# A two-layer streaming encoder trunk on one core: when the last output tiles, the late modulation sums and the layer norm's mean work are handed between the engines

## The reference, cut to what matters

```python
for layer in range(2):
    mod = silu(c) @ ada_w[layer] + ada_b[layer]
    sh1, sc1, g1, sh2, sc2, g2 = split(mod, 6)
    h = rmsnorm(x, norm_g[layer, 0]) * (1 + sc1) + sh1
    y = diff_attention(h) if layer == 0 else conformer_conv(h)
    x = x + g1 * y
    h = rmsnorm(x, norm_g[layer, 1]) * (1 + sc2) + sh2
    x = x + g2 * conv_ffn(h)
return rmsnorm(x, final_g)

def conformer_conv(h):
    a = h @ w_pw1 + b_pw1
    a = a[..., :1024] * sigmoid(a[..., 1024:])
    a = causal_dwconv(a, w_dw) + b_dw          # 31 taps for each channel
    a = silu(layernorm(a, ln_g, ln_b))
    return a @ w_pw2 + b_pw2
```

## Time and profile before

| what | us |
|---|---|
| median of 3 runs | 1253.19 |
| lowest and highest run | 1252.7, 1255.36 |
| the profiled execution | 1246.89 |
| its span | 1245.1 |
| TensorE busy in it | 1211.5 (97%) |
| VectorE, ScalarE, POOL busy | 708.4, 543.3, 541.5 |
| mean granted clock of TensorE | 0.982 of full speed |

### The profile page before, as it was taken

The page is one execution under the profiler, slowest core; times in us unless marked ns, Lnnn a source line. Parts: engine busy times, 40 slices in busy tenths (PEclk is TensorE's granted clock), DMA queues, the critical chain, the costliest instruction groups (busy, mean ns, idle before and its releaser), DMA issues.

```text
span 1245.1 us, 16710 instructions
## 1 busy us (share of the span) xinstructions
PE 1211.5 (97%) x5454; PEld 968.8 (78%) x5454; DVE 708.4 (57%) x1166; ACT 543.3 (44%) x872; POOL 541.5 (43%) x273
## 2 busy tenths in 40 slices
PE   7999999989999999999999999999999999999996
PEld 6877777767888888888888776577888888888885
DVE  5677767864767633347887899962533333340002
ACT  4356555544434434342224666753544444442221
POOL 2433323124344434454443799743444444454440
PEclk6899999899999999999999999999999999999998
DMA  9844443222655433336673212012223332222321
GB/s 358 245 143 143 152 168 118 102 102 68 203 184 171 150 102 101 101 112 228 241 241 107 85 68 68 34 39 97 83 86 101 101 101 101 91 104 93 103 83 68
DMA packets 45639, 157.04 MB, mean 126 GB/s; under 512 B 5536, under 2 KB 5792, under 8 KB 45600
## 3 DMA queue, kind: packets, MB, share of 16 engines
q1 hardware_dynamic: 44928, 156.21, 37.1%
q10 hardware_dynamic: 672, 0.34, 0.1%
HBM read 154.10 MB, written 2.42 MB: 126 GB/s over the span
## 4 chain that ended last, share of the span: by engine, by line
PE 79%; DVE 13%; issue 3%; ACT 2%; DMA 1%; POOL 1%; SPq 0%; DVEq 0%; POOLq 0%; ACTq 0%
PE psum L937 24%; PE psum L938 24%; PE psum L939 24%; DVE psum L1786 6%; PE psum L948 1%; DVE pt_lo L1516 1%; DVE psum L1507 1%; PE psum L971 1%; PE psum L1096 1%; DMA ada_first<-ada_w 1%; DVE acc L1358 1%; POOL acc_p L522 1%; PE psum L960 0%; PE psum L1123 0%; DMA w_raw<-w_tiles 0%
## 5 line engine op out<-in xcount | busy, mean ns | idle before, releaser
L509 POOL TENSOR_TENSOR w_lo<-w_raw,w_hi 128x1024 fp32r<-128x1024 f32 (+1 forms) x192 | 455.9, 2391 | 653.6 <-ACT w_hi L596 653.6
L937 PE MATMUL psum<-h_hi,w_hi 128*128 128x512 f32 x1152 | 462.1, 401 | 7.0 <-DVE x L1615 2.2
L938 PE MATMUL psum<-h_lo,w_hi 128*128 128x512 f32 x1152 | 451.4, 392 | 0.0
L939 PE MATMUL psum<-h_hi,w_lo 128*128 128x512 f32 x1152 | 451.3, 392 | 0.0
L937 PEld LDWEIGHTS psum<-h_hi,w_hi 128*128 128x128 f32 x1152 | 218.4, 190 | 56.7 <-issue 9.6
L939 PEld LDWEIGHTS psum<-h_hi,w_lo 128*128 128x128 f32 x1152 | 217.8, 189 | 46.5
L938 PEld LDWEIGHTS psum<-h_lo,w_hi 128*128 128x128 f32 x1152 | 218.1, 189 | 44.1 <-issue 1.7
L596 ACT ACTIVATE w_hi<-w_raw 128x1024 fp32r<-128x1024 f32 (+1 forms) x192 | 195.8, 1033 | 87.1 <-DMA w_raw<-w_tiles 87.0
L937 PE MATMUL psum<-a_hi,w_hi 128*128 128x512 f32 x352 | 137.1, 389 | 0.8 <-issue 0.8
L939 PE MATMUL psum<-a_hi,w_lo 128*128 128x512 f32 x352 | 136.9, 389 | 0.0
L938 PE MATMUL psum<-a_lo,w_hi 128*128 128x512 f32 x352 | 136.9, 389 | 0.0
(11 more groups left out here) (191 smaller groups left out, 1302.1 us busy)
## 6 DMA issues: line engine op xcount, KB each, us to landing
w_raw<-w_tiles SPq DMA_DIRECT2D x160, 512.0 KB, 3.3
ada_buf<-ada_w SPq DMA_DIRECT2D x32, 512.0 KB, 3.3
w_raw<-w_tiles SPq DMA_DIRECT2D x32, 448.0 KB, 3.1
ada_late<-ada_w SPq DMA_DIRECT2D x28, 512.0 KB, 5.3
ada_mid<-ada_w SPq DMA_DIRECT2D x20, 512.0 KB, 4.5
ada_first<-ada_w SPq DMA_DIRECT2D x16, 512.0 KB, 10.2
x<-x_in SPq DMA_DIRECT2D x4, 512.0 KB, 7.1
bias<-rel_scratch SPq DMA_DIRECT2D x8, 256.0 KB, 6.4
```

The costliest lines, as they stand in the source:

```text
L509: nc.gpsimd.tensor_tensor(w_lo[:, slot, 0:k], w_raw[:, (ph.tile + l) % 2, 0:k], f(w_hi[:, slot, 0:k]), ALU.subtract).then_inc(lo_done, 1)
L937: nc.tensor.matmul(dst, w_hi[:, slot, k], rhs_hi, start=first, stop=False)
L938: nc.tensor.matmul(dst, w_hi[:, slot, k], rhs_lo, start=False, stop=False)
L939: return nc.tensor.matmul(dst, w_lo[:, slot, k], rhs_hi, start=False, stop=last)
```

## The change

The constants give OUT, PW2 and the end new orders:

```diff
+LATE_ORDER, LATE_FREE = (2, 4, 1, 3), (1, 2, 3, 4, 4, 4, 5, 5)
+POOL_FINAL, FINAL_ORDER = 2, (2, 3, 0, 4, 5, 6, 1, 7)
-MORE_PE_TAPS = {4: 1, 5: 1, 6: 3, 7: 5}
+MORE_PE_TAPS = {4: 1, 5: 1, 6: 3, 7: 6}
+def pool_taps_of(t):
+    return POOL_TAPS - 1 if t == DK - 1 else POOL_TAPS
-        acc_late = at("acc_late", [P, LATE - 1, S], F32, h_base + 4 * 2 * S * 4)
+        acc_even = at("acc_even", [P, 3, S], F32, offset_of["h_lo"])
+        acc_odd = at("acc_odd", [P, 3, 3 * S], F32, offset_of["pad_v"] - 2 * 4 * 3 * S)
```

```diff
+            def last_pair(ph):
+                weights_ready(ph, 1, 1, 2)
+                for j in range(2):
+                    for k in range(DK):
+                        last = mm3(psum[:, 2 + j], slot_of(ph, 1, 2 + j), k, h_hi[:, k], h_lo[:, k], k == 0, k == DK - 1)
+                    last.then_inc(used if j else tile_used, 1)
...
-                dve.wait_ge(used, lin(i, ph.group + c + 1, 2))
+                by_tile = last and per_group == 2
+                if not by_tile:
+                    dve.wait_ge(used, lin(i, ph.group + c + 1, 2))
                 for j in range(per_group):
+                    if by_tile and j == 0:
+                        dve.wait_ge(tile_used, 1 if ph is OUT else 2)
+                    elif by_tile:
+                        dve.wait_ge(used, ph.group + 4)
```

```diff
-            attention_steps(3, 1)[14][0]()
...
             square_sum(1, 2)
-            keep_warm(12)
+            pe.wait_ge(ada_used, 8 * (CH0 + HEADS))
+            ada_product(HEAD_OUT, acc[:])
+            keep_warm(9)
```

```diff
-            for q in range(1, LATE - 1):
+            for q in LATE_ORDER:
                 last_ada(q)
...
-            last_ada(LATE - 1)
-            keep_warm(16)
+            for q in (5, 6):
+                last_ada(q)
+            keep_warm(11)
...
-                        if n == 2 and m < LATE:
-                            dve.wait_ge(ada_mm, LATE_CH + m)
+                        if n == 2:
+                            dve.wait_ge(ada_mm, LATE_CH + LATE_FREE[m - 1])
```

```diff
             act.wait_ge(delta_ready, 1)
+            nc.scalar.activation(rstd[:], delta[:], ACT.Square).then_inc(delta_squared, 1)
...
-            dve.wait_ge(delta_ready, 1)
-            V.tensor_tensor(rstd[:], delta[:], delta[:], ALU.mult).then_inc(dve_step, own.tick())
             dve.wait_ge(dsq_mm, DK)
-            dve.wait_ge(dve_step, own.now())
+            dve.wait_ge(delta_squared, 1)
...
-            late_out(LATE - 1, LATE, psum[:, LAST_OUT, 0:4])
+            late_out(5, LATE, psum[:, LAST_OUT, 0:8])
             dve.wait_ge(delta_copied, 1)
-            for m in range(DK // 2):
+            for m in range(2):
```

```diff
+            pool.wait_ge(final_gained, POOL_FINAL)
+            pool.wait_ge(rms_ready, 6)
+            for m in range(POOL_FINAL):
+                nc.gpsimd.tensor_tensor(x[:, m], x[:, m], rms[:], ALU.mult).then_inc(final_done, 1)
...
+                if n == 4:
+                    act.wait_ge(rms_ready, 5)
+                    nc.scalar.activation(rms[:], rms[:], ACT.Exp, scale=-0.5).then_inc(rms_ready, 1)
...
-                for m in range(DK):
+                for m in range(POOL_FINAL, DK):
                     V.scalar_tensor_tensor(out=x[:, m], in0=x[:, m], scalar=col("final_g", m),
```

More of the change, by code:

```diff
@@ L572, in _ @@
             pool.wait_ge(dsq_mm, DK)
-            for m in range(DK // 2, DK):
+            for m in range(2, DK):
                 nc.gpsimd.tensor_tensor(y[:, m], y[:, m], delta[:], ALU.subtract).then_inc(pool_mean, 1)
@@ L809, in residual_phase @@
                     squares(ph.bodies - 1, c, base, per_group)
+                    if ph is DOWN1 and c == 0:
+                        for m in range(POOL_FINAL):
+                            act.wait_ge(sq_ready, 4 * DK + m + 1)
+                            nc.scalar.activation(x[:, m], x[:, m], ACT.Copy, scale=col("final_g", m)).then_inc(final_gained, 1)
                     if then and c == 0:
@@ L871, in conv_group @@
                                          scale=col("w_dw", TAPS * t + tap)).then_inc(acc_started, 1)
-                for n in range(POOL_TAPS):
+                for n in range(pool_taps_of(t)):
                     b = POOL_TAPS * c + n
@@ L1645, in late_out, with head_out @@
                 dve.wait_ge(sc_read, LATE0 + MID + (1 if hi < LATE else 2))
+            def head_out():
+                dve.wait_ge(ada_mm, CH0 + HEADS)
+                at_, b = 4 * (CH0 + HEADS - 1), PARAMS["ada_b"] + 4 * (CH0 + HEADS - 1)
+                V.tensor_tensor(mod[:, at_:at_ + 4], psum[:, HEAD_OUT, 0:4], prm[:, b:b + 4], ALU.add)\
+                 .then_inc(dve_step, own.tick())
             def up(layer):
@@ L1700, in _ @@
                     residual(i, c, OUT, 0, 2, GATE[0], last=2 * i + c == 3)
+            head_out()
             norm(1)
```

45 lines of the change are left out of this document (26 added, 19 removed).

## The result

| us | before | changed |
|---|---|---|
| median of the runs | 1253.19 (1251.01 to 1257.56, 5 runs) | 1245.59 (1243.59 to 1247.62, 5 runs) |
| ratio to before, 95% interval | | 0.9934 (0.9915 to 0.9953) |
| profiled execution: time, span, mean clock | 1246.89, 1245.1, 0.982 | 1245.94, 1244.2, 0.979 |

The change makes the kernel 0.66% faster, by 7.6 us. The two profiled executions differ by only 0.95, and the first thing to explain is why: the last head's mean square, up to which nothing is changed but a few addresses, came at 264.42 before and 268.11 in the changed kernel. From there on the changed kernel took 4.6 us less. So each stretch is compared by itself, and never against the start of the span.

The account below looks back on a forecast made before the run. TensorE, busy 97% of the span, was taken as the bound, with gains only at six waits: 2.9 + 0.85 + 0.35 + 1.3 + 0.85 + 1.3 = 7.55 us, so 1253.19 - 7.55 = 1245.6 us; range 1242.0 to 1249.5.

Parts of the forecast that it names:

- A: Behind the attention: last modulation product moved behind OUT, so TensorE waits less for VectorE's first residual; 2.9 us, bounds 2.2 to 3.2.
- B: Behind OUT: last pair done tile by tile, leaving one tile's channel sum behind the last residual; 0.85 us, bounds 0.6 to 1.0.
- C: Ahead of PW1: four late products instead of five, TensorE then waits for the first `h_lo`; 0.35 us.
- D: Layer norm ahead of PW2: shorter POOL sum, square on ScalarE, fewer VectorE subtractions, Silu earlier; 1.3 us, bounds 0.3 to 1.5.
- E: Behind PW2: last pair done tile by tile as behind OUT, without the moved product; 0.85 us.
- F: Last norm and stores: VectorE does six tiles, POOL two, so the last store is issued earlier; 1.3 us, bounds 0.5 to 1.3.
- C's clock term: At PW1's start: clock falls again as before, 3.4 us at half speed losing 1.7 in both kernels; otherwise at most 1.6 gained.
- the clock gives more: Rival, 0.22: no fall at PW1, or A's gap had cost timed runs a slow stretch; gain 8.8 to 10.4, about 1243.5.
- The handovers stay: Rival, 0.20: D held by late products or a clock fall before PW2, or F's stores wait for POOL; gain 4 to 6.
- Not as it says: Rival, 0.06: earlier starts wait for loads or the convolution; only F and some of A left; gain up to 2.5.
- Slower: Rival, 0.02: clock stays at 1.2 GHz behind a new or moved wait, 20 us more at the low level; 1256.

Follow-up runs that it names:

- the second series: The changed kernel run once more without an edit, beside the kernel before: 1247.26 us (8 runs) for 1253.27, ratio 0.9955.

## Why the prediction was right, and where not

The time, 1245.6 forecast, came out at 1245.59 and, when the same kernel was run again, at 1247.26. The agreement to 0.01 is luck, as the parts show. Those behind it, from the pair of profiles:

| part | forecast | measured | |
|---|---|---|---|
| A | 2.9 | 2.83 | as worked out |
| B | 0.85 | 0.85 | as worked out |
| C | 0.35, clock as before | first product 0.29 earlier, first `u_pad` 0.93 later by a longer fall | the size of the clock's share was off |
| D | 1.3 | 1.32 | as worked out |
| E | 0.85 | 0.80 | as worked out |
| F | 1.3 | 0.0 | failed |
| sum | 7.55 | 6.1 without the clock | |

**A, B, E** went by the steps named: the product off VectorE's path, one tile's sum behind the last residual, `head_out` and its product in the shadow of the factor (the 0 that was taken for it, against up to 0.3).

**D** held link by link: last sum 0.19 earlier where 0.1 was reckoned, variance 0.64 for 0.75, Silu 1.30 for 1.35. The reading that TensorE's ninth tap leaves little of POOL's shorter sum was right, and is priced by the kernel without it: 0.32. The row was right to be set against the rule on table loads: with VectorE out of the way, Silu starts 1.41 behind the start of the load (818.00, 819.41), not 2.66. The Trainium skill, ScalarE: Activation LUTs, What ACT_TABLE_LOAD costs, has 2.66 with the drain; by it D would have given nothing, and the trace disagrees.

**F is the step that failed.** It was: "the last store is issued with the last of them, and the span ends 2.65 later. Six end 1.3 earlier, at 1241.15." The 2.65 was taken for a fixed delay behind the last issue. It is a queue: the transfer engines are full from the first store on, and the last store waits in them. From VectorE's last tile to the end it was 4.0. The last store was issued 0.76 earlier behind the first factor and landed at the same 7.62; the median landing took 2.6 us for 2.2. Nor could it be issued 1.3 earlier: by the prediction's own 0.62 from one issue to the next, eight issues that begin 0.77 behind the factor put the last at 5.1, for 5.38 before (here it came at 4.62). The rows for it were there to be asked for: the share and GB/s of the transfer engines by stretches of half a microsecond. And both bounds, 0.5 and 1.3, lay above nothing though no row excluded nothing.

**C's clock term** was of the right kind and mis-sized. Of "the clock falls again, as before: 3.4 us at half speed lose 1.7" the length held in three of the five profiles that have C's order and one-column products (19.15 to 19.39); in the other two it was 6.8 us (20.56 and 20.65). A fall of 3.4 us there cost 1.0 to 1.5 against the kernels without a fall, not 1.7, and the next 3.4 another 1.2 to 1.5. That no more than 1.6 can be had by a clock that stays up came out: 1.48 and 1.55 less than before (18.15 and 18.08).

**Why the sum still came out.** 6.1 us of parts against 7.6 between the first medians, 6.0 in the second series and 7.0 over all runs. The rival "the clock gives more" named a source for the excess: the falls behind A's gap. They exist, 1.5 to 1.6 us in four of six profiles with the empty gap and in none of the seven with part A, about 1.0 us on the mean. That would be enough for the 0.9 between 6.1 and 7.0. But the runs speak against the clock as the whole answer: the mean clock of the 13 runs of the changed kernel is 0.9788, and so is that of the 95 of before. What the falls behind A's gap gave back may have been lost elsewhere, as in C's longer fall, and then they explain no excess. Where the 0.9 comes from stays open. At PW2's start the clock fell in six of the eight profiles that don't have C and D both, and in two of the six that do, 1.5 us mostly; so few can't settle whether the change helps there. So the number was right by two errors that offset one another: 1.3 of F that is missing, and an excess over the parts that it didn't hold (1.5 in the first series, 0.9 over all runs, none in the second). Five parts of six hold, C's without its clock.

**The other rivals.** "The handovers stay", with a gain of 4 to 6, is touched by the second series' 6.0, but its mechanism fell with D's and B's rows; its one true piece was F, for another reason (transfers, not POOL: POOL was done at 1239.4). "Not as it says" has nothing for it. "Slower" has only C's longer fall for it, which cost 1.2 us and not the 10 that it needs.

**The gain of 0.95 between the two profiles** is no measure, and the prediction's 1239.3 for the profiled execution was missed by 6.6: it set out from 1246.89, a lucky execution, and 3.7 us went to the stretch ahead of the mean square, where the clock was at 0.86 between 250 and 275 us for 1.00 before. Kernels with and without the change show both (mean square at 264.3 to 269.9), so it isn't the change's.

## What to carry to other kernels

Before crediting an earlier last issue, look at what the transfer engines do in stretches of half a microsecond: where they are full from the first store to the last, an earlier last issue gave nothing here. What an earlier first store is worth stays open, as the one kernel that had it let them run dry behind it. Here the clock fell behind a row of one-column products although TensorE was shown busy; the same products made wide, where the bank had room, took the same time and kept the clock, so it is worth trying where a fall follows such a row. And price the parts of a change in stretches between two events that it doesn't touch, since the times of one and the same kernel spread here over 11 us, along with the clock.

## What was not expected of the hardware

- Forty float32 product rows with 128 weights take 4.52 us with one column and 4.59 with 80, and TensorE's next product starts 4.38 behind the first of them in both; thirty-two take 4.0 with one and 3.9 with 96.
- Behind one-column products, or during them, the clock fell about PW1's start in all eleven profiles that have them there (3.4 to 10 us at 1.2 GHz) and in none of the three that have wide ones or products of ones.
- Stores of 256 KB run at 373 to 393 GB/s with all transfer engines full; the Trainium skill, DMA: Bandwidth & Descriptors, Where 436 GB/s comes from, gives about 358 as a core's share of the memory and 435 as the fabric's ceiling. The trace, with one core at work, lies between the two, above the first.
- The times of the kernel before in 95 runs go with the mean clock of the run: 11 us from the fastest to the slowest, 0.974 to 0.983.
